# Copies of values and keys ahead of weight loads, and half of two modulations on ScalarE

## The reference

```
mod = silu(c) @ w_ada + b_ada            # shift, scale, gate, twice
h   = rmsnorm(x, g_norm1) * (1 + sc1) + sh1
proj = h @ w_in                          # q, k, v of 8 stick-breaking and 8 chunked heads
o_sb = stick_breaking_attention(q_sb, k_sb, v_sb)
o_ca = chunked_relpos_attention(rmsnorm(q_ca, g_q), rmsnorm(k_ca, g_k), v_ca)
x = x + gt1 * (concat(o_sb, o_ca) @ w_o)
h = rmsnorm(x, g_norm2) * (1 + sc2) + sh2
x = x + gt2 * (square(relu(h @ w1)) @ w2)
```

## Time and profile before

| what | value |
|---|---|
| median of 3 runs | 981.45 us (981.32 to 982.88) |
| the profiled execution, its own time | 983.12 us |
| its span, first to last instruction | 981.3 us |
| PE busy | 959.3 us, 98% |
| DVE busy | 686.3 us, 70% |
| ACT busy | 538.6 us, 55% |
| mean granted clock of PE | 0.998 |

### The profile page before, as it was taken

How to read it: one execution, slowest core, us unless ns; L and a number is a source line. 1 busy time by engine, 2 the same in 40 slices (tenths; PEclk the granted TensorE clock), 3 DMA queues, 4 the chain that set the end, 5 groups by cost and what they waited for, 6 DMA issues and landing times.

```text
span 981.3 us, 13125 instructions
## 1 busy us (share of the span) xinstructions
PE 959.3 (98%) x4712; PEld 800.2 (82%) x4712; DVE 686.3 (70%) x1269; ACT 538.6 (55%) x1053; POOL 83.2 (8%) x173
## 2 busy tenths in 40 slices
PE   8999999999999999999989999999999999999998
PEld 7878998878888888777777887788888888888886
DVE  6487888868788759767668886966644853774773
ACT  6448777753223345489877563446645634644520
POOL 4000001011122012100000000110000001000000
PEclk9999999999999999999999999999999999999999
DMA  8205222238787425644433323446777567473201
GB/s 298 82 24 185 66 76 87 81 145 335 298 318 281 173 108 188 241 92 154 111 119 92 102 65 136 158 112 153 180 221 178 171 201 191 115 224 129 85 33 54
DMA packets 36673, 148.69 MB, mean 152 GB/s; under 512 B 9193, under 2 KB 9193, under 8 KB 24706
## 3 DMA queue, kind: packets, MB, share of 16 engines
q1 hardware_dynamic: 23970, 101.41, 29.6%
q0 software_dynamic: 9568, 42.48, 16.5%
q10 hardware_dynamic: 3072, 3.98, 1.2%
HBM read 138.32 MB, written 5.27 MB: 146 GB/s over the span
## 4 chain that ended last, share of the span: by engine, by line
PE 81%; DVE 9%; ACT 4%; DMA 3%; issue 2%; POOL 0%; SPq 0%; ACTq 0%; DVEq 0%; POOLq 0%
PE psum L2092 24%; PE psum L2094 24%; PE psum L2093 24%; PE psum L2259 3%; PE psum L2238 2%; PE psum L2288 1%; DVE wl L1237 1%; PE psum L2291 1%; DMA raw<-in_wall 1%; DVE two L1776 1%; DMA value_rows<-rows 1%; DVE hl L1277 1%; DVE two L1641 1%; DMA al<-al 1%; DVE xt L1273 1%
## 5 line engine op out<-in xcount | busy, mean ns | idle before, releaser
L2092 PE MATMUL psum<-hh,wh 128*128 128x512 f32 (+1 forms) x720 | 274.2, 381 | 0.7 <-DVE hl L1277 0.6
L2094 PE MATMUL psum<-hh,wl 128*128 128x512 f32 (+1 forms) x720 | 267.4, 371 | 0.0
L2093 PE MATMUL psum<-hl,wh 128*128 128x512 f32 (+1 forms) x720 | 267.4, 371 | 0.0
L1237 DVE TENSOR_TENSOR wl<-raw,wh 128x512 fp32r<-128x512 f32 x328 | 213.8, 683 | 45.6 <-ACT wh L698 45.3
L698 ACT ACTIVATE wh<-raw 128x512 fp32r<-128x512 f32 x328 | 188.8, 620 | 84.1 <-PE psum L2094 68.2
L2092 PEld LDWEIGHTS psum<-hh,wh 128*128 128x128 f32 x720 | 135.4, 188 | 24.3 <-DVE hl L1277 1.5
L2094 PEld LDWEIGHTS psum<-hh,wl 128*128 128x128 f32 x720 | 135.3, 188 | 23.7
L2093 PEld LDWEIGHTS psum<-hl,wh 128*128 128x128 f32 x720 | 135.6, 188 | 21.1 <-issue 1.0
L2092 PE MATMUL psum<-wh,ah 128*128 128x512 f32 x224 | 88.5, 395 | 0.0
L2094 PE MATMUL psum<-wh,al 128*128 128x512 f32 x224 | 87.4, 390 | 0.0
L2093 PE MATMUL psum<-wl,ah 128*128 128x512 f32 x224 | 87.3, 390 | 0.0
(11 more groups left out here) (335 smaller groups left out, 1632.5 us busy)
## 6 DMA issues: line engine op xcount, KB each, us to landing
raw<-in_wall SPq DMA_DIRECT2D x78, 1024.0 KB, 5.1
raw<-in_wall POOLq DMA_DIRECT2D x15, 1024.0 KB, 7.9
wa<-in_wada POOLq DMA_DIRECT2D x24, 512.0 KB, 6.1
gt<-in_wada POOLq DMA_DIRECT2D x20, 512.0 KB, 6.1
xt<-in_xcols SPq DMA_DIRECT2D x8, 264.0 KB, 8.2
cb<-c_rows SPq DMA_DIRECT2D x8, 264.0 KB, 3.2
x<-in_x SPq DMA_DIRECT2D x4, 512.0 KB, 10.1
x_kept<-x SPq DMA_DIRECT2D x4, 512.0 KB, 2.8
```

Source lines behind the costliest of these rows:

```text
L1237: e.tensor_tensor(home(w)[1][:, cs], raw_of(w, c), home(w)[0][:, cs].bitcast(F32), ALU.subtract).then_inc(v["wl"], 1)
L2092: e.matmul(out_, lh, rh, start=start, stop=False, skip_group_check=True)
L2093: e.matmul(out_, lh, rl, start=False, stop=False, skip_group_check=True)
L2094: return e.matmul(out_, ll, rh, start=False, stop=stop, skip_group_check=True)
```

## The change

It has five parts.

1. The values' copies of the first 256 tokens (m = 4) are issued ahead of the weight load of that turn, and the copy of the zero row one turn earlier.
2. In turns 1 to 4 SP waits, before the weight load, until the key copies of this turn have landed.
3. DVE's and ACT's steps on the first two blocks of values move from steps 87 to 90 to steps 90 to 94.
4. POOL's `gate_rows` and `gate(0)` move from the tables of head 9 to behind PE's twelfth product of queries and keys, which ends at step 127.
5. In both norms ACT does the second half of each modulation (`modulate`, 4 instructions of 128x128 with scale and bias from memory, on the bank of b = 1), ahead of its two roundings in its queue. DVE keeps the half b = 0.

```diff
-        DV, DV_UPPER, DV_LOWER = (87, 88, 113, 122), (88, 89, 114, 123), (89, 90, 115, 124)
+        DV, DV_UPPER, DV_LOWER = (90, 92, 113, 122), (91, 93, 114, 123), (92, 94, 115, 124)
...
-                loads_to(W_CA + m + 1 + NR)
-                if m == 4:
+                if m == 3:
                     for j in range(4):
                         e.wait_ge(d[f"x{4 + j}"], 32)
 
                     e.wait_ge(g["strip"], 1)
                     e.dma_start(v_mem[0:1, :], dv[0][0:1, :]).then_inc(d["vm0"], 16)
+                if m == 4:
                     values_out(0)
                     values_out(1)
                     values_before(0)
                     values_before(1)
+                if 1 <= m < 5:
+
+                    e.wait_ge(d[f"kd{(3 + m) % 2}"], 64 * ((3 + m) // 2) - 64)
+                loads_to(W_CA + m + 1 + NR)
...
+            def modulate(i, s_):
+
+                n = 4 * s_ + i
+                e.wait_ge(t["tp"], n + 1)
+                if i:
+                    e.wait_ge(v["hl"], 2 * n)
+                else:
+                    e.wait_ge(v["ada"], s_ + 1)
+                    e.wait_ge(*((v["qn"], 8) if s_ else (v["ml"], 8)))
+                src = bank[(TURN_BANK_2 if s_ else TURN_BANK)[i % 2][1]]
+                for k in range(4):
+                    ins = e.activation(two[:, 1, 128 * k:128 * k + 128], src[:, 128 * k:128 * k + 128], ACT.Identity,
+                                       bias=mod[:, 24 * s_ + 4 + k:24 * s_ + 5 + k], scale=cols[:, s_, 4 + k:5 + k])
+                ins.then_inc(a["mod"], 1)
...
             squares(2, 0)
             squares(2, 1)
+            modulate(0, 0)
             h_upper(0, 0)
             h_upper(0, 1)
...
             squares_2(1, 2)
+            modulate(1, 1)
             h_upper_2(1, 0)
             h_upper_2(1, 1)
+            modulate(2, 1)
             h_upper_2(2, 0)
             h_upper_2(2, 1)
...
                     e.memset(dv[0][0:1, :], 0.0).then_inc(g["strip"], 1)
-                    gate_rows()
-                    gate(0)
...
+            e.wait_ge(t["pq"], 12)
+            gate_rows()
+            gate(0)
```

More of the change, by code:

```diff
@@ L313, in program @@
                  "nsq", "xk", "hh", "vca", "sq", "ln", "sq_s", "vsb", "r", "r2", "sh", "acc",
-                 "exp", "norm", "sig", "dv", "turn", "o", "oh")
+                 "exp", "norm", "sig", "dv", "turn", "o", "oh", "mod")
         v = sems("dve_", "wl", "acc", "ss0", "dg", "xn0", "hl0", "hn", "wfl", "v", "f", "scan", "crow", "cc", "za", "u", "y", "yz", "yl", "m",
@@ L992, in keep @@
                 e.activation(x1[:, i, :], scaled[:, i % 2, :], ACT.Copy, scale=sm[:, 128 + 2 * i:129 + 2 * i]).then_inc(a["xk"], 1)
+            def modulate(i, s_):
[11 more added lines that the diff above has]
+                ins.then_inc(a["mod"], 1)
             def h_upper(i, b):
-                e.wait_ge(v["t1"], 2 * i + b + 1)
+                e.wait_ge(*((a["mod"], i + 1) if b else (v["t1"], i + 1)))
                 if i == 0 and b == 0:
@@ L1024, in _ @@
             squares(3, 1)
+            modulate(1, 0)
             h_upper(1, 0)
@@ L1029, in _ @@
             vca(0)
+            modulate(2, 0)
             h_upper(2, 0)
@@ L1033, in _ @@
             vca(1)
+            modulate(3, 0)
             h_upper(3, 0)
@@ L1115, in h_upper_2 @@
             def h_upper_2(i, b):
-                e.wait_ge(v["t2"], 2 * i + b + 1)
+                e.wait_ge(*((a["mod"], 4 + i + 1) if b else (v["t2"], i + 1)))
                 e.activation(hh[:, 4 * b:4 * b + 4, META + 128 * i:META + 128 * i + 128],
@@ L1129, in _ @@
             squares_2(1, 1)
+            modulate(0, 1)
             h_upper_2(0, 0)
@@ L1141, in _ @@
             upper(W_MLP + 1, 1)
+            modulate(3, 1)
             h_upper_2(3, 0)
@@ L1629, in norms, with h_mod @@
                                 ALU.mult).then_inc(v["xn1"], 1)
-            def h_mod(i, b):
+            def h_mod(i):
                 e.wait_ge(t["tp"], i + 1)
                 if i:
-                    e.wait_ge(v["hl"], 2 * i + b - 1)
-                elif b == 0:
+                    e.wait_ge(v["hl"], 2 * i - 1)
+                else:
                     e.wait_ge(v["ada"], 1)
@@ L1639, in h_mod @@
                 for k in range(4):
-                    kt = 4 * b + k
-                    ins = e.tensor_scalar(two[:, b, 128 * k:128 * k + 128], bank[TURN_BANK[i % 2][b]][:, 128 * k:128 * k + 128],
-                                          cols[:, 0, kt:kt + 1], mod[:, kt:kt + 1], ALU.mult, ALU.add)
+                    ins = e.tensor_scalar(two[:, 0, 128 * k:128 * k + 128], bank[TURN_BANK[i % 2][0]][:, 128 * k:128 * k + 128],
+                                          cols[:, 0, k:k + 1], mod[:, k:k + 1], ALU.mult, ALU.add)
                 ins.then_inc(v["t1"], 1)
@@ L1668, in _ @@
             scale(2)
-            h_mod(0, 0)
-            h_mod(0, 1)
+            h_mod(0)
             h_lower(0, 0)
@@ L1676, in _ @@
             norms(2)
-            h_mod(1, 0)
-            h_mod(1, 1)
+            h_mod(1)
             h_lower(1, 0)
@@ L1683, in _ @@
             vca(0)
-            h_mod(2, 0)
-            h_mod(2, 1)
+            h_mod(2)
             h_lower(2, 0)
@@ L1689, in _ @@
             vca(1)
-            h_mod(3, 0)
-            h_mod(3, 1)
+            h_mod(3)
             h_lower(3, 0)
@@ L1764, in norm_2, with h_mod_2 @@
                                 ALU.mult).then_inc(v["xn2"], 1)
-            def h_mod_2(i, b):
+            def h_mod_2(i):
                 e.wait_ge(t["tp"], 4 + i + 1)
                 if i:
-                    e.wait_ge(v["hl"], 8 + 2 * i + b - 1)
-                elif b == 0:
+                    e.wait_ge(v["hl"], 8 + 2 * i - 1)
+                else:
                     e.wait_ge(v["ada"], 2)
@@ L1774, in h_mod_2 @@
                 for k in range(4):
[L1775 to L1778, removed]
+                    ins = e.tensor_scalar(two[:, 0, 128 * k:128 * k + 128],
+                                          bank[TURN_BANK_2[i % 2][0]][:, 128 * k:128 * k + 128],
+                                          cols[:, 1, k:k + 1], mod[:, 24 + k:25 + k], ALU.mult, ALU.add)
                 ins.then_inc(v["t2"], 1)
@@ L2227, in score @@
                     else:
-                        e.wait_ge(v["t1"], 8)
+                        e.wait_ge(v["t1"], 4)
+                        e.wait_ge(a["mod"], 4)
                 elif c > 66:
@@ L2438, in turn_block @@
                 else:
-                    e.wait_ge(v["t1"], 2 * i - 2)
+                    e.wait_ge(v["t1"], i - 1)
+                    e.wait_ge(a["mod"], i - 1)
                 for kt in range(8):
@@ L2534, in turn_2 @@
                 if i > 1:
-                    e.wait_ge(v["t2"], 2 * i - 2)
+                    e.wait_ge(v["t2"], i - 1)
+                    e.wait_ge(a["mod"], 4 + i - 1)
                 for kt in range(8):
```

12 lines of the change are left out of this document (4 added, 8 removed).

## The result

The changed kernel takes **988.25 us** in the median of 4 runs (987.83 to 988.89), the kernel before 981.38 (980.17 to 982.88) beside it: a ratio of 1.0077, 95% interval 1.0056 to 1.0098. It is slower by 6.9 us, where 3.7 us less than before were forecast. The profiled execution took 988.15 us, 5.0 more than that of before.

What follows compares the result with a forecast made beforehand. PE was taken as the bound, busy 959.3 of 981.3 us. Values 4.7 + keys 1.4 - first norm 1.1 + second norm 0.3 = 5.3 off the profiled 983.12 gave 977.8 us; range 975.2 to 980.3.

Steps and rivals of the forecast that it cites:

- Moved to about 540 us, the gate leaves the copy to land after 2.2 to 2.8 us: Head 10's last key copy, 5.01 us before, lands at 443.4 once the gate's 512 KB read is gone; PE's wait ends.
- The gate's first reader: The sum behind the output projection, 33 steps after PE's twelfth product, so the moved gate comes in time; no cost counted.
- the slower one: Rival: ACT becomes the bound in the norms, its instructions costing 4.0 us and table loads 2.6; 984.4 us, chance 0.05.
- The keys, 1.4: Head 10's scores: PE's 1.4 us wait for the last key copy goes; bounds 0 and 1.4.
- SP's own wait: SP holds weights back 2 to 3 us for the keys; adds little either way, the weights being two units ahead of use.
- The values, 4.7: Near 494 to 501 us: PE's 3.0 us wait for ptl goes, and 1.7 us of lower clock behind it.
- took 1.67 off for the median: The median lies 1.67 us below the profiled execution; most runs were taken to lack the lower-clock stretch, leaving a 3.7 gain.
- The first norm, -1.1: ACT's half of the modulations delays the first norm: a loss of 1.1 us, bounds 0.3 and 1.8.
- The second subtraction: First norm, first block: DVE's subtraction ends at 374.9 instead of 373.95, making PE 0.95 us late.
- The second block: First norm: the same chain, entered 0.8 us later, makes the low half 1.1 us late, which holds the 0.95.
- The second norm, +0.3: Sharing modulations with ACT gains 0.1 us at the third block and 0.2 at the last.
- the cheap bound: ACT's four modulation instructions at a spacing of 0.29, 1.26 us instead of 1.58; the second norm then gains 1.4 us.

Runs made afterwards that it cites:

- e1: Changed kernel with both gate_rows writes and the read into gt put back at head 9; 980.45 us, ratio to before 0.9957.
- e6: Changed kernel with gate_rows written in 128 pieces of 16 bytes instead of 512 of 4, gate values in wrong order; 977.36 us, ratio to before 0.9941.
- e14: Kernel before with only the gate changed: wide pieces, quiet place, order put right by GpSimd; 978.97 us, ratio to before 0.9986.
- e3: Changed kernel with the two gate_rows writes back at head 9, only the 512 KB read into gt left late; 977.69 us, ratio to before 0.9942.
- e11: e9 without the waits on kd ahead of the weight loads; 978.2 us.
- e8: Kernel before with only the waits on kd added, the gate's 4-byte writes still at head 9; 981.76 us, ratio to before 0.9984.
- e15: e14 with the value part of the change alone added; 976.2 us, ratio to before 0.9954.
- e12: e9 with the first norm's modulations all on VectorE; 977.9 us.
- e17: e13 with the first norm's modulations all on VectorE; 975.44 us.
- e18: e13 with the second norm's modulations all on VectorE; 976.65 us.
- e13: Changed kernel with wide gate pieces in the quiet place, order put right by GpSimd on one partition before the read; 975.44 us, ratio to before 0.995.
- e5: Changed kernel with gate_rows held until pair 9's key copies landed, the read until pair 10's; 979.8 us, ratio to before 0.9958.
- e9: Changed kernel with wide gate pieces, writes after pair 9's copies, read after pair 10's, VectorE reading gt strided; 978.11 us, ratio to before 0.9968.

## Why the prediction was wrong

**The step that failed** is "Moved to about 540 us, the gate leaves the copy to land after 2.2 to 2.8 us", with what follows it: "The gate's first reader is the sum behind the output projection, ... so it comes in time". It priced the moved gate by its own arrival and looked only at the place that it left. What `gate_rows` would meet at the new place wasn't asked, so the sum has no term for it; and of the gate's transfers only the 512 KB read was counted, not the two writes ahead of it. The gate also comes earlier than the 540 us given, at 528.05. A sign could be read beforehand: the earlier trace rows has the read waiting 11.73 us for a write of 2 KB. In place of nothing the runs showed 10.9 us of PE's wait and 2.3 us more for the stretch at the lower clock, gone with the writes back (e1) and nearly gone with wide ones (e6). None of the rivals had it; the slower one put its chance on ScalarE, which was never near.

**The keys, 1.4: right size, cause open.** The wait went, as the trace of the changed kernel shows, and it goes in the old order of SP's queue too once the gate is elsewhere (e14), so it was the gate's. The trace of the kernel before has only the copies behind the read slow, which is the prediction's reading; e3 has a like wait with no read, but with the weights behind the second write. SP's own wait was said to add little in either direction: with wide pieces that holds (e11), beside the 4-byte writes it doesn't, since it moves a load of weights behind one of them (e1, e3, e8). That engines take turns between queues, as cited, led to GpSimd's queue, and the read was the only transfer looked at in it.

**The values, 4.7: right mechanism, partly right size.** In the changed kernel the copies go out ahead of the weights and VectorE idles for no DMA there. First the timeline of SP's queue, then the landing times of line L614 beside the earlier trace rows:

```profile
478.35 4.78 SPq L614 DMA_DIRECT2D value_rows<-rows  x4
483.17 1.96 SPq L624 DMA_DIRECT2D x<-value_rows  x2
485.22 0.86 SPq L549 DMA_DIRECT2D raw<-in_wall  x1
```

```profile
DMA to landing us min/median/max: 2.1/2.2/2.3
```

The reads back are issued at 483, well before the forecast's 489, and PE is busy without a gap from 480 to 500 at full clock. Between profiled executions the part gives 4.1 us (e14, e15), at the medians 2.8. The prediction has 4.7 for the profiled execution and took 1.67 off for the median, so 3.0: the stall isn't the same in every run, as it suspected.

**The first norm, -1.1: too dear.** e12 and e17 put it at 0 to 0.2 us of time, the waits at 0.3. The second subtraction was said to be 0.95 late at 374. In the trace of the changed kernel PE waits 0.45 there. The second block was said to hold this and come 1.1 late; PE waits 0.33 us for it, where the kernel before waited 0.48. So the walk's delays don't reach the second block. ScalarE runs its half and both roundings without a gap, as the walk has it, in somewhat less time. The line of the modulations, by duration in ns, and their timeline:

```profile
L1009 ACT ACTIVATE two<-psum,mod,cols x32: 440/458/486, 371.2 to 653.7; 128x128 f32<-128x128 f32 x32
```

```profile
371.21 1.49 ACT L1009 ACTIVATE two<-psum,mod,cols 128x128 f32<-128x128 f32 x4
372.59 1.15 ACT L1017 ACTIVATE hh<-two 128x512 fp32r<-128x512 f32 x2
```

One takes 458 ns (467 estimated) and four 1.49 us (1.58 estimated): the price of the instruction was about right, and the 1.64 cited beside it further off; no load of a table is added to the six of the kernel before. **The second norm, +0.3, was too low**: 0.9 by the waits, 1.0 to 1.2 by e18 beside e17, where the cheap bound gave 1.4. Which step of that walk was too dear isn't worked out.

**The sum.** From e14 to e13, which is the change without its gate, the profiled executions fall by 4.4 us (980.31 to 975.89); the prediction's terms for the same are 4.7 - 1.1 + 0.3 = 3.9. At the medians it is 3.5, where the prediction, less its 1.67, has 2.2. To this the gate adds -1.7 for what it no longer costs near heads 9 and 10 (e14 against before) and +13.2 for head 18, from the trace of the changed kernel: 981.4 - 3.5 - 1.7 + 13.2 = 989.4, against 988.25 measured. The 1.1 us between them is less than what separates the groups of runs.

## What to carry to other kernels

Price a moved transfer at the place where it arrives, not only at the one that it leaves, and price each issue of it: a write of 2 KB can be the dearest thing on the DMA engines. The sign of it in a profile is a small transfer with a long time to landing, and, where it does harm, a DMA share near 1 at a few tens of GB/s beside it. Look too at what a new wait in a queue moves: here it put a load of weights behind such a write. Write such a row in pieces as wide as the layout allows, and put the order right on an idle engine, on one partition.

## What the runs showed of the hardware

- 512 pieces of 4 bytes from GpSimd's queue took 8.3 to 14.5 us to land (before, e5), 10.9 in the median of the changed kernel's two; 128 pieces of 16 bytes took 1.7 (e6).
- A 1 MB load of weights issued 0.5 to 1.3 us behind such a write landed after 13.9 to 17.2 us (changed kernel, e1, e3, e8), issued 0.5 or 1.4 us ahead of one after 7.3 and 7.2 (e5, before); the median of that line is 5.0. 128 KB copies behind the held load in the same queue took 13.7 instead of 2.3 (changed kernel), but 3.2 and 2.6 beside a write with no load ahead of them (before).
- Much of the kernel's spread from run to run went with these transfers: in one group before had 7 us (26 runs, 977.99 to 984.84), with wide pieces in a quiet place 3.5 (e14, 12 runs), with the values ahead of the weights too 0.4 (e15, 9 runs).
- VectorE's 128x512 product of PSUM with a tile read at a stride of 16 bytes took 1062 ns (e9), side by side 684 (changed kernel).
